# adaLN product by rows of the weights, with a transpose on VectorE, and a reordered beginning

## The chip, the cores and the metric

The kernel runs on one core of a Trainium2 chip. The metric is the device time of one execution in microseconds (us); the median of several executions is compared. The core has TensorE (PE, matmuls; its weight loads are PEld in the profile), VectorE (DVE), ScalarE (ACT), GpSimd (POOL) and SyncE (SP, which here issues most transfers). Each engine works through its own queue in order, and the queues wait for each other through semaphores.

## The reference

One inference step of a small diffusion backbone of two layers on 128 context tokens (prompt) and 128 latent tokens (sample), width 1024, all in float32. Every layer has a token mixer (layer 0 a bidirectional gated recurrence with 8 heads, layer 1 neighbourhood attention) and a mixture of 64 experts with 6 chosen per token. Before each of the four sub-layers stands an RMS norm with adaLN modulation:

```
def _modulation(cvec, ada_w, ada_b):          # cvec: c_ctx for the prompt, c for the sample
    m = silu(cvec) @ ada_w + ada_b            # (1024) @ (1024, 6144)
    return split(m, 6)                        # shift, scale, gate of the mixer; shift, scale, gate of the experts
h = rmsnorm(x, norm_w) * (1 + scale) + shift  # before each sub-layer
x = x + gate * sublayer(h)
```

The change concerns this product (two layers of six parts of 1024 columns, for two condition vectors), and the order in which the first things are loaded and computed.

## The kernel before

Activations lie transposed in SBUF: `xT` and `hT` are 128 partitions x 8 blocks x 256 tokens, and row p*8+k of a width-1024 vector lies on partition p in block k. Weights come through five rooms (`stage`) of 2 MB each, the "stage loads", in a fixed order: four adaLN halves, then the ten 512-column blocks of the recurrence's input projection ("in") with one or two adaLN halves behind each, as the list `ROUNDS` has it, 34 loads in all. SP issues load n as soon as load n-5 has been used (`block_used`). A round is: projection b on PE (`project`), the recurrence's steps that the list puts at its middle and at its end (`recur`), and the adaLN halves (`ada`). The other engines walk through the same list in their own queues. After the rounds come the recurrence's last steps, the output projection (`project_out`), the experts of layer 0 (`experts_front`, `experts`, a loop over 32 pairs of experts), then layer 1.

adaLN part n = (layer, j) is computed in steps:
- A stage load has all 1024 rows of 512 columns (half a part); rows of the load are 2 KB. `ada(n)` on PE multiplies it with the condition vectors (`cond_act`, padded to 32 columns): 8 matmuls of 512 columns, in four column tiles of 32 that each sum two of the eight blocks. All results lie in PSUM bank 7.
- `ada_rows` on ACT copies the bank to `mrow`; PE waits for this (`ada_row`) before the next half.
- When both halves are copied, `ada_columns` on PE turns the row into columns and sums the four tiles: 8 matmuls with 128x128 weights cut from `mrow` and two moving columns (`sel`).
- `modulation` on DVE adds `ada_b` and, for the scale parts, forms the `gain`. The next part's `ada` waits for it (`mod_done`).

In the rounds, `ada_columns` of a part stands in the middle of the projection in a later round (`midway`), and `modulation` stands on DVE between the recurrence's middle and end steps.

The beginning: SP loads both token groups, then every second entry of the list `small` (condition vectors, norm weights, biases, decay bounds, router weights and biases), then stage loads 0 to 4, the table of masks, and after `lb_ps` the states. ACT issues the identity and the other half of `small`. One semaphore counts all of `small`. ACT (Silu of the condition) and PE (transposes of the decay bound logits, `lb_ps`) wait for all of it. PE then sums the squares for the first norm (`norm_sums`) and computes parts 0 and 1; the first projection follows the first norm, which needs these parts. Each matmul in float32 appears in the trace as two records, each with its weight load.

Of the kernel before, what the change touches and what calls it, by code (L numbers as in the profile page):

```python
# [46 lines left out]
C_ID, C_SEL, C_MASKF, C_MASKB, C_BEFORE, C_IOTA, C_WIN, C_WNEG, C_FLIP, C_END = np.cumsum(  # L47
    [0, 128, 2, 128, 32, 128, 4 * SLOTS, 128, 128, 128]).tolist()


def shape_constants():
# [8 lines left out]
    for g in range(4):  # L60
        for s in range(2):
            c[32 * g + s, C_SEL + s] = 1.0
# [9 lines left out]
def build(nc, io):  # L72
    ctx = ExitStack()
    with ctx:
# [106 lines left out]
        mrow = sc(D, (D,))  # L181
# [28 lines left out]
        sel = consts[:, C_SEL:C_SEL + 2]  # L210
# [8 lines left out]
        s_const, s_x, s_small, s_s0 = sem("consts_in"), sem("x_in"), sem("small_in"), sem("states_in")  # L219
        stage_in = [sem(f"stage_in{n}") for n in range(5)]  # L220
# [6 lines left out]
        ada_ps, ada_row, sel_ps, mod_done = sem("ada_in_psum"), sem("ada_rows"), sem("ada_cols_in_psum"), sem("mod_done")  # L227
# [96 lines left out]

        def block_used(n):
# [4 lines left out]
        SMALL = 12 * 16  # L330
# [4 lines left out]
        def heads(a, g):  # L335
# [4 lines left out]
            (cond[:, 0, :], io["c_ctx"].rearrange("(p k) -> p k", p=P)),  # L340
            (cond[:, 1, :], io["c"][0].rearrange("(p k) -> p k", p=P)),
# [5 lines left out]
            (gn_w, io["hgrn_gn_w"].rearrange("a d -> d a")),  # L347
            (router_w[:, 0], io["moe_w_router"][0].rearrange("(p k) e -> p k e", p=P)),
# [4 lines left out]
        assert len(small) * 16 == SMALL  # L353
# [3 lines left out]
        def _(sp):  # L357
            sp.dma_start(x_tok[:, 0, :], io["x_prompt"][0]).then_inc(s_x, 16)
            sp.dma_start(x_tok[:, 1, :], io["x_sample"][0]).then_inc(s_x, 16)
            for dst, src in small[0::2]:  # L360
                sp.dma_start(dst, src).then_inc(s_small, 16)

            def load_stage(n):

                sp.dma_start(stage[rooms[n]], stage_source(stages[n])).then_inc(stage_in[rooms[n]], 16)
# [131 lines left out]
        def _(act):  # L497
            act.dma_start(consts[:, 0:C_MASKF], io["table"][:, 0:C_MASKF]).then_inc(s_const, 16)
            for dst, src in small[1::2]:
# [129 lines left out]
            for b, middle, end, _, adas in ada_rounds():  # L629
# [4 lines left out]
                for n in adas:  # L634
                    ada_rows(n)
# [1090 lines left out]
```

## Time and profile before

| what | value |
|---|---|
| median of the runs | 1677.94 us (3 runs, 1677.0 to 1679.94) |
| the profiled execution: time, span | 1678.47 us, 1676.7 us |
| PE busy | 1604.1 us, 96% of the span |
| weight loads (PEld) | 1150.6 us, 69% |
| DVE, ACT, POOL busy | 468.4, 458.7, 18.6 us |
| mean granted TensorE clock | 0.968 of full speed |
| bytes moved, mean rate | 510.50 MB, 304 GB/s |
| stage loads of ada_w, of the input projection | 24 and 10, of 2048 KB each |
| router loads | weights 2 x 256 KB, biases 2 x 32 KB |

The profile is one execution. Busy time of PE is time in which a matmul was in the pipe, at whatever clock was granted; the clock stands beside it. Times in the rows are from the start of the span.

### The profile page before, as it was taken

The numbers are of one execution on the slowest core, as the hardware profiler recorded it, in microseconds if no ns is written. First come the engines' busy times: TensorE is split into PE (matmuls) and PEld (weight loads), VectorE is DVE, ScalarE is ACT, GpSimd is POOL, SyncE is SP. The second block draws the span as 40 slices with busy tenths as digits, with TensorE's granted clock in tenths as the row PEclk, the third lists the DMA queues.
The fourth block names the chain that finished last, engine by engine and source line by source line (L and its number), as shares of the span: only waits on it lengthen the run. The fifth ranks groups of instructions, "written<-read, shape, count | busy, mean of one in ns | idle before, by whom it ended". The sixth has DMA issues, their size and how long they took to land.

```text
span 1676.7 us, 30416 instructions
## 1 busy us (share of the span) xinstructions
PE 1604.1 (96%) x13039; PEld 1150.6 (69%) x13039; DVE 468.4 (28%) x857; ACT 458.7 (27%) x1055; POOL 18.6 (1%) x25
## 2 busy tenths in 40 slices
PE   5999999989999999999998998989999999999996
PEld 3767866776767767676775775857676767667674
DVE  1035035142222222222222216152222222222224
ACT  2223222231222232222222204132322222222223
POOL 0000000010000000000000000020000000000000
PEclk9999898889999999999999899989999999999999
DMA  9867585663999999999999244237999999999980
GB/s 326 315 240 263 195 284 179 259 226 131 372 389 383 384 388 384 392 385 385 388 383 388 56 151 174 67 163 302 386 381 391 384 391 383 385 387 383 391 340 27
DMA packets 130113, 510.50 MB, mean 304 GB/s; under 512 B 11256, under 2 KB 19600, under 8 KB 97296
## 3 DMA queue, kind: packets, MB, share of 16 engines
q1 hardware_dynamic: 124832, 506.23, 78.5%
q10 hardware_dynamic: 5232, 3.57, 0.7%
q8 instruction: 37, 0.61, 0.1%
q14 instruction: 12, 0.10, 0.0%
HBM read 506.64 MB, written 3.15 MB: 304 GB/s over the span
## 4 chain that ended last, share of the span: by engine, by line
PE 92%; DVE 4%; ACT 3%; DMA 1%; issue 1%; ACTq 0%; DVEq 0%
PE psum L1230 90%; ACT arena L503 1%; PE psum L1551 1%; DMA arena<-in_moe_router_bias 1%; DVE arena L802 0%; DVE arena L844 0%; ACT arena L526 0%; ACTq L500 0%; DVE arena L1064 0%; ACT arena L743 0%; ACT L514 0%; PE psum L1698 0%; DVE arena L804 0%; DVE arena L1123 0%; DVE arena L1119 0%
## 5 line engine op out<-in xcount | busy, mean ns | idle before, releaser
L1230 PE MATMUL psum<-arena 128*64 128x256 f32 (+9 forms) x12756 | 1573.9, 348 | 42.8 <-ACT arena L526 14.3
L1230 PEld LDWEIGHTS psum<-arena 128*64 128x64 f32 (+3 forms) x12756 | 1120.5, 141 | 488.9 <-issue 278.1
L503 ACT ACTIVATE arena<-psum 128x512 f32<-128x512 f32 (+4 forms) x514 | 217.2, 440 | 508.3 <-PE psum L1230 402.6
L1119 DVE TENSOR_TENSOR arena<-psum,arena 128x512 f32<-128x512 f32 x128 | 88.1, 689 | 285.5 <-ACT arena L503 285.5
L503 ACT ACTIVATE arena<-arena 128x512 bf16<-128x512 f32 (+1 forms) x144 | 87.6, 618 | 111.7 <-DVE arena L1119 109.0
L1123 DVE TENSOR_TENSOR arena<-arena 128x512 bf16<-128x512 f32 x128 | 88.7, 693 | 98.1 <-ACT arena L503 98.1
L1110 DVE SCALAR_TENSOR_TENSOR arena<-arena,psum 128x256 f32<-128x256 f32 x64 | 30.8, 482 | 277.6 <-ACT arena L676 277.6
L676 ACT ACTIVATE arena<-psum 128x256 f32<-128x256 f32 x64 | 24.7, 386 | 298.2 <-PE psum L1230 298.2
L1104 DVE COPY arena<-psum 128x512 f32<-128x512 f32 x64 | 44.4, 693 | 136.1 <-PE psum L1230 136.1
L824 DVE TENSOR_TENSOR arena<-psum,arena 128x16 f32<-128x16 f32 x12 | 2.1, 175 | 144.4 <-PE psum L1230 144.4
L844 DVE SCALAR_TENSOR_TENSOR arena<-psum,arena 128x128 f32<-128x128 f32 x64 | 17.7, 344 | 65.3 <-PE psum L1230 65.3
L510 ACT ACTIVATE arena<-arena 128x512 f32<-128x512 f32 x20 | 12.3, 630 | 73.3 <-DVE arena L844 73.2
L492 POOL TENSOR_TENSOR arena<-arena 128x512 f32<-128x512 f32 (+1 forms) x16 | 16.9, 1089 | 1092.9 <-ACT arena L503 1092.8
L1551 PE MATMUL psum<-arena 128*128 128x128 f32 x128 | 25.0, 277 | 2.0 <-DVE arena L1110 2.0
L1031 DVE TENSOR_TENSOR arena<-arena 128x256 bf16<-128x256 f32 x64 | 26.6, 416 | 0.0
L503 ACT ACTIVATION_READ_ACCUMULATOR arena<-psum 64x1 f32 x128 | 25.1, 196 | 0.8
L560 ACT ACTIVATE arena<-psum 128x1024 f32<-128x1024 f32 x8 | 8.2, 1026 | 57.3 <-PE psum L1230 57.3
L526 ACT ACTIVATE arena<-arena 128x128 f32<-128x128 f32 x32 | 12.8, 480 | 12.4 <-DVE arena L804 7.8
L1551 PEld LDWEIGHTS psum<-arena 128*128 128x128 f32 x128 | 13.0, 142 | 2.9 <-DVE arena L1110 2.9
L925 DVE TENSOR_TENSOR arena<-arena 128x1024 f32<-128x1024 f32 x12 | 14.1, 1220 | 0.1
L802 DVE RECIPROCAL arena<-arena 128x256 f32<-128x256 f32 x5 | 8.8, 1754 | 13.8 <-ACT arena L514 13.8
L804 DVE TENSOR_TENSOR arena<-arena 128x512 f32<-128x512 f32 (+1 forms) x15 | 12.1, 865 | 0.2
(137 smaller groups left out, 297.6 us busy)
## 6 DMA issues: line engine op xcount, KB each, us to landing
arena<-in_moe_w_gate SPq DMA_DIRECT2D x64, 2048.0 KB, 9.5
arena<-in_moe_w_up SPq DMA_DIRECT2D x64, 2048.0 KB, 14.1
arena<-in_moe_w_down SPq DMA_DIRECT2D x64, 2048.0 KB, 10.5
arena<-in_ada_w SPq DMA_DIRECT2D x24, 2048.0 KB, 14.9
arena<-in_hgrn_w_in SPq DMA_DIRECT2D x10, 2048.0 KB, 13.6
arena<-in_na_w_qkv SPq DMA_DIRECT2D x6, 2048.0 KB, 19.3
arena<-in_hgrn_w_out SPq DMA_DIRECT2D x1, 4096.0 KB, 13.0
arena<-in_na_w_o SPq DMA_DIRECT2D x1, 4096.0 KB, 14.0
```

Source lines behind the costliest of these rows:

```text
L492: pool.tensor_tensor(out, h_rest[:, a, ks], h_tok[:, part, a, ks], ALU.subtract)\
L503: return act.activation(out, in_, ACT.Copy, **kw)
L676: act.activation(silu[:, j], psum[:, 4, 0:F], ACT.Silu).then_inc(M.silu, 1)
L844: ins = dve.scalar_tensor_tensor(out=xT[:, k, at], in0=psum[:, k // 2, (k % 2) * NT + s * T:(k % 2) * NT + (s + 1) * T], scalar=g[:, k, s: ...
L925: ins = dve.tensor_tensor(dif[d].rearrange("p u (b t) -> p (u b) t", t=size), view, view[:, :, at:at + 1].broadcast_to(shape), ALU.subtract)
L1031: dve.tensor_tensor(onehot[:, j].rearrange("p a (e s) -> p a e s", e=2), slots.unsqueeze(1).unsqueeze(1).broadcast_to(shape), ranks.unsque ...
L1104: dve.tensor_copy(xg[:, j, 4:8], psum[:, 7, :].rearrange("p (k t) -> p k t", t=P)).then_inc(M.xg[1], 1)
L1110: dve.scalar_tensor_tensor(out=hid[:, j], in0=silu[:, j], scalar=slot_w[:, j:j + 1], in1=psum[:, 4, F:2 * F], op0=ALU.mult, op1=ALU.mult). ...
L1119: dve.tensor_tensor(y_rest[:, ds], psum[:, 6 + half, :], y[:, j, 0, ds], ALU.subtract)\
L1123: ins = dve.tensor_tensor(y[:, j, 2, ds], y_rest[:, ds], y[:, j, 1, ds], ALU.subtract)
L1230: return pe.matmul(out, lhsT, rhs, start=start, stop=stop, skip_group_check=True, **kw)
L1551: ins = pe.transpose(psum[:, 5, c * P:(c + 1) * P], hid[:, j, c * P:(c + 1) * P], ident)
```

## The change

It puts the product in another form and moves loads and steps at the beginning:
- A stage load of a half has 512 rows (four of the eight blocks k) of all 1024 columns, in rows of 4 KB. PE multiplies it in 16 matmuls of 256 columns: four column tiles, each with its own quarter of the columns, summed over k in both halves. The sum is complete in 32 partitions x 256 columns per tile.
- `ada_rows`, `ada_columns` and `sel` are gone. DVE transposes bank 7 in blocks of 32x32 into `mod_rows` and adds `ada_b` to two of the 32 columns. PE waits for the transpose (`mod_turned`) before the next part's first half; there is no wait between halves.
- Condition vectors are loaded first, on a semaphore of their own (`s_cond`). All other small loads go to ACT's queue; router weights and biases go to SP's queue behind stage load 9, on `s_router`; the table goes behind load 6 and the states behind load 8 (after `lb_ps`).
- PE transposes the decay bound logits after the first four halves. DVE does the first norm and parts 0 and 1 ahead of the decay bounds, and ACT likewise. PE waits for table and routers ahead of the first router product, DVE for the routers where it adds the bias.

```diff
             if what[0] == "ada":
                 _, l, j, half = what
-                src = io["ada_w"][l, :, j * D + half * BLOCK:j * D + (half + 1) * BLOCK]
+                src = io["ada_w"][l, :, j * D:(j + 1) * D].rearrange("(p k) n -> p k n", p=P)
+                return src[:, half * K // 2:(half + 1) * K // 2]
...
         def _(sp):
+            sp.dma_start(cond[:, 0, :], io["c_ctx"].rearrange("(p k) -> p k", p=P)).then_inc(s_cond, 16)
             sp.dma_start(x_tok[:, 0, :], io["x_prompt"][0]).then_inc(s_x, 16)
             sp.dma_start(x_tok[:, 1, :], io["x_sample"][0]).then_inc(s_x, 16)
-            for dst, src in small[0::2]:
-                sp.dma_start(dst, src).then_inc(s_small, 16)
...
             for n in range(5):
                 load_stage(n)
-            sp.dma_start(consts[:, C_MASKF:], io["table"][:, C_MASKF:]).then_inc(s_table, 16)
-            sp.wait_ge(lb_ps, 1)
-            for d, name in enumerate(("state_hgrn_fwd", "state_hgrn_bwd")):
-                sp.dma_start(s0[:, d], io[name][0, 0].rearrange("h k v -> k h v")).then_inc(s_s0, 16)
             for n in range(5, stages0):
                 sp.wait_ge(*block_used(n - 5))
                 load_stage(n)
+                if n == 6:
+                    sp.dma_start(consts[:, C_MASKF:], io["table"][:, C_MASKF:]).then_inc(s_table, 16)
+                if n == 8:
+                    sp.wait_ge(lb_ps, 1)
+                    for d, name in enumerate(("state_hgrn_fwd", "state_hgrn_bwd")):
+                        sp.dma_start(s0[:, d], io[name][0, 0].rearrange("h k v -> k h v")).then_inc(s_s0, 16)
+                if n == 9:
+                    for dst, src in routers:
+                        sp.dma_start(dst, src).then_inc(s_router, 16)
...
         def _(act):
+            act.dma_start(cond[:, 1, :], io["c"][0].rearrange("(p k) -> p k", p=P)).then_inc(s_cond, 16)
             act.dma_start(consts[:, 0:C_MASKF], io["table"][:, 0:C_MASKF]).then_inc(s_const, 16)
-            for dst, src in small[1::2]:
+            for dst, src in small:
                 act.dma_start(dst, src).then_inc(s_small, 16)
...
-            def ada_rows(n):
-
-                act.wait_ge(ada_ps, n + 1)
-                if n % 2 == 0 and n >= 2:
-                    act.wait_ge(sel_ps, n // 2)
-                copy(mrow[:, (n % 2) * BLOCK:(n % 2 + 1) * BLOCK], psum[:, 7, :]).then_inc(ada_row, 1)
-
-            act.wait_ge(s_small, SMALL)
+            act.wait_ge(s_cond, 32)
             act.wait_ge(ready, 5)
...
             squares(0)
+            norm_root(0)
+            act.wait_ge(s_small, SMALL)
+            norm(0, mod[:, 0, 0])
             act.wait_ge(lb_shift, 1)
             act.activation(lb, lb, ACT.Exp).then_inc(lb_exp, 1)
-            norm_root(0)
-            for n in range(4):
-                ada_rows(n)
-            norm(0, mod[:, 0, 0])
...
             def modulation(n):
 
                 l, j = parts[n]
-                dve.wait_ge(sel_ps, n + 1)
-                dve.tensor_tensor(mod[:, l, j], psum[:, 7, 0:2 * K].rearrange("p (k s) -> p k s", s=2),
+                dve.wait_ge(ada_ps, 2 * n + 2)
+                if n >= 2:
+                    dve.wait_ge(mod_done, n - 1)
+                dve.transpose(mod_rows[:, n % 2],
+                              psum[:, 7, 0:NT].rearrange("p (q k) -> p k q", k=K))\
+                   .then_inc(mod_turned, 1)
+                dve.wait_ge(mod_turned, n + 1)
+                dve.tensor_tensor(mod[:, l, j], mod_rows[:, n % 2, :, 0:2],
                                   ada_b[:, l, j].unsqueeze(2).broadcast_to((P, K, 2)), ALU.add).then_inc(mod_done, 1)
...
             def ada(n):
 
                 w = staged()
-                if n % 2:
-                    pe.wait_ge(ada_row, n)
-                elif n:
-                    pe.wait_ge(mod_done, n // 2)
-                for i in range(K // 4):
+                part, half = n // 2, n % 2
+                if half == 0 and part:
+                    pe.wait_ge(mod_turned, part)
+                for i in range(K // 2):
                     for c in range(4):
-                        ins = mm(psum[32 * c:32 * c + 32, 7, :], cond_act[:, 4 * i + c, :], w[:, 4 * i + c, :],
-                                 i == 0, i == K // 4 - 1)
+                        ins = mm(psum[32 * c:32 * c + 32, 7, 0:NT], cond_act[:, half * K // 2 + i, :],
+                                 w[:, i, c * NT:(c + 1) * NT], half == 0 and i == 0, half == 1 and i == K // 2 - 1)
                 ins.then_inc(ada_ps, 1)
 
-            def ada_columns(n):
-
-                pe.wait_ge(ada_row, 2 * n + 2)
-                for k in range(K):
-                    ins = mm(psum[:, 7, 2 * k:2 * k + 2], mrow[:, k::K], sel, True, True)
-                ins.then_inc(sel_ps, 1)
-
-            for n in range(2):
-                ada(2 * n)
-                ada(2 * n + 1)
-                ada_columns(n)
-            pe.wait_ge(s_table, 16)
+            for n in range(4):
+                ada(n)
+            pe.wait_ge(s_small, SMALL)
+            for i in range(3):
+                ins = pe.transpose(psum[:, 5, i * HEADS:(i + 1) * HEADS], lbrow[0:HEADS, i], ident[0:HEADS, 0:HEADS])
+            ins.then_inc(lb_ps, 1)
...
                         recur(g, item)
-                    if part is not None:
-                        ada_columns(part)
...
+            pe.wait_ge(s_table, 16)
+            pe.wait_ge(s_router, ROUTER)
             experts_front(0)
```

## Rows read from the trace of the kernel before

**Rows 1.** Windows: length, busy PE PEld DVE ACT POOL (count), clock, DMA share, GB/s.
```profile
2.00:14.00 12.00, 3.65 (x16) 3.28 (x16) 1.61 (x3) 1.28 (x1) 0.23 (x2) 1.00 1.00 285
14.00:36.00 22.00, 14.86 (x67) 10.26 (x68) 5.94 (x14) 7.84 (x13) 0.00 (x0) 1.00 1.04 386
48.55:295.19 246.64, 243.05 (x1521) 177.57 (x1521) 75.00 (x106) 66.55 (x86) 0.00 (x0) 0.91 0.68 245
48.55:64.80 16.25, 16.25 (x68) 13.63 (x72) 1.17 (x5) 3.45 (x7) 0.00 (x0) 0.86 1.02 376
64.80:80.70 15.90, 15.90 (x85) 12.53 (x88) 0.00 (x0) 1.62 (x2) 0.00 (x0) 1.00 0.78 274
500.00:600.00 100.00, 100.00 (x972) 69.82 (x970) 25.11 (x42) 27.65 (x72) 0.00 (x0) 1.00 0.98 388
```

**Rows 2.** Chain of waits, 0 to 60 us: start, length, what.
```profile
6.12 11.62 DMA arena<-in_moe_router_bias
...
29.06 1.96 PE psum L1230 x16
...
31.70 3.98 PE psum L1230 x16
...
36.02 3.61 PE psum L1230 x16
...
48.55 11.51 PE psum L1230 x42
```

**Rows 3.** The fifth stage load (first projection): issue time, and time to landing.
```profile
L365 SPq DMA_DIRECT2D arena<-in_hgrn_w_in x1: 5295/5295/5295, 20.3 to 20.3; - x1
...
DMA to landing us min/median/max: 20.1/20.1/20.1
```

**Rows 4.** Windows: behind the third columns; the first and last low-clock columns.
```profile
94.10:97.50 3.40, 3.40 (x10) 2.72 (x9) 3.33 (x10) 1.06 (x1) 0.00 (x0) 0.51 0.02 4
139.50:143.50 4.00, 4.00 (x19) 4.00 (x18) 0.04 (x1) 0.00 (x0) 0.00 (x0) 0.78 1.05 387
...
275.20:279.20 4.00, 4.00 (x26) 3.99 (x18) 0.00 (x0) 0.00 (x0) 0.00 (x0) 0.89 1.05 391
```

**Rows 5.** Groups by form, PE, 48.55 to 295.19 us: busy, mean | idle before.
```profile
L1230 PE MATMUL psum<-arena 128*32 128x512 f32 x273 | 33.3, 598 | 1.6 <-ACT arena L503 1.6
L1230 PE MATMUL psum<-arena 128*128 128x2 f32 x128 | 30.9, 372 | 0.2 <-PE psum L1369 0.2
L1230 PE MATMUL psum<-arena 128*128 128x128 f32 x80 | 9.9, 278 | 1.8 <-DVE arena L969 1.8
```

**Rows 6.** Timeline of PEld in the second projection: start, length, what.
```profile
66.59 13.68 PEld L1230 LDWEIGHTS psum<-arena 128*128 128x128 f32 x64 [0.84 <-issue]
```

**Rows 7.** Timeline of PEld in an expert's gate and up product.
```profile
707.38 6.62 PEld L1230 LDWEIGHTS psum<-arena 128*64 128x64 f32 x62 [0.29 <-issue]
```

**Rows 8.** Groups by form, PEld and DVE, beginning to the output projection.
```profile
L1230 PEld LDWEIGHTS psum<-arena 128*32 128x32 f32 x768 | 15.7, 111 | 30.6 <-issue 30.2
L824 DVE TENSOR_TENSOR arena<-psum,arena 128x16 f32<-128x16 f32 x12 | 2.1, 175 | 144.4 <-PE psum L1230 144.4
L802 DVE RECIPROCAL arena<-arena 128x256 f32<-128x256 f32 x1 | 1.8, 1754 | 3.3 <-ACT arena L514 3.3
L964 DVE TENSOR_TENSOR arena<-psum,arena 128x256 f32<-128x256 f32 x2 | 0.8, 414 | 0.0
```

**Rows 9.** Chain of waits, 295 to 320 us.
```profile
295.26 1.90 PE psum L1230 x16
...
297.83 3.98 PE psum L1230 x16
...
302.16 3.65 PE psum L1230 x16
...
307.74 1.11 ACT arena L619
...
308.88 1.28 ACT L622
...
310.17 1.06 ACT arena L622
...
312.82 7.59 PE psum L1230 x28
```

More of the change, by code:

```diff
@@ L44 @@
 BLOCK_W = K * BLOCK
-C_ID, C_SEL, C_MASKF, C_MASKB, C_BEFORE, C_IOTA, C_WIN, C_WNEG, C_FLIP, C_END = np.cumsum(
-    [0, 128, 2, 128, 32, 128, 4 * SLOTS, 128, 128, 128]).tolist()
+C_ID, C_MASKF, C_MASKB, C_BEFORE, C_IOTA, C_WIN, C_WNEG, C_FLIP, C_END = np.cumsum(
+    [0, 128, 128, 32, 128, 4 * SLOTS, 128, 128, 128]).tolist()
 def shape_constants():
@@ L59, in shape_constants @@
     c[:, C_IOTA:C_IOTA + 4 * SLOTS] = np.arange(4 * SLOTS)[None, :]
-    for g in range(4):
-        for s in range(2):
-            c[32 * g + s, C_SEL + s] = 1.0
     start = np.clip(np.arange(GRID_W) - WIN_C // 2, 0, GRID_W - WIN_C)
@@ L180, in build @@
         scan_keep = sc(UNITS * T)
-        mrow = sc(D, (D,))
+        mod_rows = sc(2 * K * 32, (2, K, 32))
         x_tok = cut(2 * D, (2, D), at=scratch_at)
@@ L209, in build @@
         before = consts[:, C_BEFORE:C_BEFORE + P]
-        sel = consts[:, C_SEL:C_SEL + 2]
         window = consts[:, C_WIN:C_WIN + P]
@@ L219, in build @@
         s_const, s_x, s_small, s_s0 = sem("consts_in"), sem("x_in"), sem("small_in"), sem("states_in")
+        s_cond, s_router = sem("cond_in"), sem("routers_in")
         stage_in = [sem(f"stage_in{n}") for n in range(5)]
@@ L226, in build @@
         cond_done = sem("cond_act_done")
-        ada_ps, ada_row, sel_ps, mod_done = sem("ada_in_psum"), sem("ada_rows"), sem("ada_cols_in_psum"), sem("mod_done")
+        ada_ps, mod_turned, mod_done = sem("ada_in_psum"), sem("mod_turned"), sem("mod_done")
         sq_done, ssum, root = sem("squares"), sem("square_sums"), sem("root")
@@ L323, in build, with stage_room @@
         room_count = [rooms[:n + 1].count(rooms[n]) for n in range(len(rooms))]
+        def stage_room(n):
+            room = stage[rooms[n]]
+            if stages[n][0] == "ada":
+                return room.rearrange("p k n -> p (k n)").rearrange("p (k n) -> p k n", n=D)
+            return room
         def block_used(n):
@@ L328, in block_used @@
             return (ada_ps, ada_n) if stages[n][0] == "ada" else (proj, n + 1 - ada_n)
-        SMALL = 12 * 16
+        SMALL, ROUTER = 6 * 16, 4 * 16
         def bank(n, count=1):
@@ L347, in build @@
             (gn_w, io["hgrn_gn_w"].rearrange("a d -> d a")),
+        ]
+        routers = [
             (router_w[:, 0], io["moe_w_router"][0].rearrange("(p k) e -> p k e", p=P)),
@@ L352, in build @@
         ]
-        assert len(small) * 16 == SMALL
+        assert (len(small) * 16, len(routers) * 16) == (SMALL, ROUTER)
         @block.sync
         def _(sp):
+            sp.dma_start(cond[:, 0, :], io["c_ctx"].rearrange("(p k) -> p k", p=P)).then_inc(s_cond, 16)
             sp.dma_start(x_tok[:, 0, :], io["x_prompt"][0]).then_inc(s_x, 16)
             sp.dma_start(x_tok[:, 1, :], io["x_sample"][0]).then_inc(s_x, 16)
-            for dst, src in small[0::2]:
-                sp.dma_start(dst, src).then_inc(s_small, 16)
             def load_stage(n):
-                sp.dma_start(stage[rooms[n]], stage_source(stages[n])).then_inc(stage_in[rooms[n]], 16)
+                sp.dma_start(stage_room(n), stage_source(stages[n])).then_inc(stage_in[rooms[n]], 16)
             def load_gate_up(m, j, expert):
@@ L627, in recur @@
                     state_out(g, 1)
-            for b, middle, end, _, adas in ada_rounds():
+            for b, middle, end, _, _ in ada_rounds():
                 for g, item in middle + end:
@@ L633, in _ @@
                     project(b)
-                for n in adas:
-                    ada_rows(n)
             def experts_front(m):
@@ L855, in _ @@
                                 psum[:, n, :].rearrange("p (k t) -> p k t", t=T)).then_inc(x_sb, 1)
+            normed(0)
             dve.wait_ge(s_small, SMALL)
+            modulation(0)
+            modulation(1)
+            gains_ready(0)
+            norm(0, mod[:, 0, 0])
             dve.wait_ge(lb_ps, 1)
@@ L868, in _ @@
             link(dve.tensor_scalar(one_minus_lb, lb0, -1.0, 1.0, ALU.mult, ALU.add))
-            normed(0)
-            modulation(0)
-            modulation(1)
-            gains_ready(0)
-            norm(0, mod[:, 0, 0])
             dve.wait_ge(s_table, 16)
@@ L1042, in experts_front @@
                 dve.wait_ge(M.scores, 1)
+                dve.wait_ge(s_router, ROUTER)
                 link(dve.tensor_tensor(selv, scores, router_b[:, m].unsqueeze(1).broadcast_to((P, 2, E)), ALU.add))
@@ L1238, in _ @@
                 ins.then_inc(x_ps, 1)
-            pe.wait_ge(s_small, SMALL)
-            for i in range(3):
-                ins = pe.transpose(psum[:, 5, i * HEADS:(i + 1) * HEADS], lbrow[0:HEADS, i], ident[0:HEADS, 0:HEADS])
-            ins.then_inc(lb_ps, 1)
             pe.wait_ge(ready, 5)
@@ L1398, in recur @@
                     state(g, 1)
-            for b, middle, end, part, adas in ada_rounds():
+            for b, middle, end, _, adas in ada_rounds():
                 def midway():
```

4 lines of the change are left out of this document (1 added, 3 removed).

## The prediction

> **What bounds the kernel now.** I read the windows by stage first, to see which engine is full where. In the expert stretches TensorE (PE) is busy for all of 100 us at a granted clock of 1.00 while transfers run at 388 GB/s [rows 1]: there PE sets the pace, and what comes earlier in time only shifts it. The change touches the first 319 us alone, so the question is what ends last there. From 48.55 us (first matmul of the first projection) to 295.19 us PE is busy for 243.05 of 246.64 us, but at a mean clock of 0.91, and the DMA engines only for 0.68 of the time [rows 1]. That stretch is PE's too, so PE time taken out of it is gained, as long as transfers don't take over.
>
> Next the chain of waits in order of time, for the beginning [rows 2]. The first conditioning matmuls wait for the last router bias (11.62 us); then each adaLN part goes PE, ScalarE (ACT) copy, PE, VectorE (DVE). The last step on PE, the "columns" product, takes 3.98 us for 16 matmuls of two columns each. The first projection starts at 48.55, although its weights, the fifth stage load, were there at 20.3 + 20.1 = 40.4 us [rows 3].
>
> Last, the granted clock around the columns [rows 4]. The stretch 94.1 to 97.5, which follows the columns of the third part, was at 0.51, so at the 1.2 GHz level; a round with a conditioning half and no columns (64.8 to 80.7) was at 1.00 [rows 1].
>
> **The change, part by part.** The profiled execution took 1678.47 us (span 1676.7), 0.5 above the median of the runs shown; sums go from it.
>
> *Columns removed.* Between 48.55 and 295.19 there were 128 two-column records, 16 for each of 8 parts [rows 5]. One set lies on the chain for 3.98 us [rows 2]. PE has no other work in that time, so all is gained: 8 x 3.98 = 31.8 us. The other four sets lie in the beginning and the tail, below.
>
> *Clock given back.* A mean of 0.91 means that 18% of 246.64 us, 44.4 us, were at half clock; half of that, 22.2 us, is lost. The first projection's own share stays (0.86 over 16.25 us: 4.6 us low, 2.3 lost [rows 1]), since PE will still have been mostly idle before it. In four of the eight column stretches the low clock already began under the columns (0.78 for the first, 0.89 for the last; together 6.3 us, 3.1 of loss) [rows 4], and that time is counted with the columns. Left: 22.2 - 2.3 - 3.1 = 16.8 us. Rounding of 0.91 makes it 15.6 to 18.0.
>
> *Row copies removed.* Two halves stood directly behind each other in two of these rounds and waited for the ACT copy: 1.6 us. PE also waited 1.8 us for the score mask, because the ACT decay exponentials were queued behind a row copy, and 0.2 before a column set [rows 5]. Together 3.6 us; those exponentials no longer have a row copy ahead of them.
>
> *The new product.* A half is now 16 matmuls of 256 columns instead of 8 of 512, each recorded as two. Four column tiles ran side by side before: 16 records of 512 took 1.90 us [rows 9]. At full clock a 256-column record takes 13.68 / 64 = 0.214 us [rows 6]; 32 of them in four tiles are 8 x 0.214 = 1.71 us, and the same remainder of 0.19 gives 1.90 again: zero. The new thing is twice as many weight loads, with half the time to hide each. The nearest row is the expert product, also 256 columns, in two tiles: 62 loads in 6.62 us, 0.214 us per pair [rows 7], so loads of twice the width are hidden there. I take zero. Above: 768 loads of this form were busy 15.7 us [rows 8], and the new product has 24 x 32 = 768: +15.7 us if all of them stood open, +7.9 for the added half. Below zero nothing: the streamed columns are the same in number.
> The Trainium skill, "TensorE: Matmul & The Clock Gate", Part 3, section "The mechanism", says that a weight load overlaps with matmuls in flight only when its row group differs. Here all four tiles use all rows, so by that rule the loads would stand open and the forecast would rise to about 1621; the expert row speaks against it.
>
> *The DVE transpose.* Not in the trace. 128x256 out of PSUM took 0.414 us as a product; the dearest DVE operation of that size, the reciprocal, 1.754, and the small add that it joins 0.175 [rows 8]. I take 0.41 and keep 0.2 to 1.75. It adds a DVE step between one part and the next part's first half, but DVE sat idle before every modulation, 144.4 us over 12 [rows 8], and both halves of a part are now ready a round before DVE comes to it. So it costs nothing in the rounds. DVE work behind it (decays, output copies) starts no later, since the wait for the columns is gone. It is on the path twice: before the first projection and in the tail.
>
> *The beginning.* Condition vectors come on a semaphore of their own, so ACT no longer waits until 17.7 us; the decay bounds leave the path. What ends last is then the fifth stage load. Four router transfers (0.59 MB) leave the queue ahead of it: 1.5 us at 386 GB/s. From 2 to 14 us only 285 GB/s were moved, a loss of 3.1 us against 386 [rows 1]; the small vectors, ada_b above all, stay, so I give back 1.2. It lands at 40.4 - 2.7 = 37.7 (35.8 to 40.4). The other arm: the fourth load lands one load (5.4 us) earlier, at 32.3; a half takes 1.9 to 3.6 us by clock [rows 2]; from the last columns to the first projection it took 1.6 us, now 2.0 with the transpose: 36.2 to 37.9. So the first projection starts at about 38.1 instead of 48.55: 10.4 us (8 to 12.5). The rows of ada_w are now read 4 KB at a time instead of 2 KB; 2 KB rows already moved 386 GB/s [rows 1], so nothing for that.
> Moved behind stages 6, 8 and 9 on SP's queue: table, states, router weights. States are wanted in the sixth round, routers past 320 us. DVE waits for the table ahead of its first decay step, which comes with the third round, near 72 us; behind loads 5 and 6 the table lands near 37.7 + 2 x 5.4 + 1.2 = 50 us. SP now waits for lb_ps behind load 8, but load 9 needs the first projection to end in any case. PE meets the table and router waits only ahead of the first router product.
>
> *The tail* (from 295.2 until the output projection, at about 318.7, where the state ends within the last chain row) loses two column sets and three row copies [rows 9]. New chain: half 1.9, transpose and wake 0.6, half 1.9 (DVE's add, gain and output copy lie beside it), ACT's square 1.1, sums 1.7, Ln 1.11, table 1.28, Exp 1.06, copy 0.6, key turn 0.7, copy 0.6, state 0.9: 13.4 us instead of 23.5. Short idle gaps remain and the clock may fall in them, so I take 10.0 (7 to 12). The last transfer needed, 4 MB of output weights, is issued ahead of this stretch and lands well within it.
>
> *Do transfers take over?* A full round loads 6.29 MB, 16.3 us at 386 GB/s; PE needs 15.9 + 1.9 = 17.8 us [rows 1, 9] and more with recurrence work. PE stays last, by 1.5 us.
>
> Sum: 10.4 + 31.8 + 16.8 + 3.6 + 10.0 = 72.6 us. 1678.5 - 72.6 = 1605.9; less 0.5 for the median: **1605**.
>
> **The rivals.**
> (a) *Open weight loads*: 7.9 to 15.7 us given back, 1613 to 1621. For it: twice the loads. Against it: the expert product. Chance 0.09.
> (b) *Transfers pace the rounds*: if loads fall under 6.29 MB / 17.8 us = 353 GB/s, as in the first 14 us, the two rounds without recurrence work stretch first. At 330 a round is 19.1 us; with a late fifth load some 8 us in all: 1613. Chance 0.07.
> (c) *The low clock belongs to the recurrence matmuls* and stays: 16.8 us are not gained, 1622. For it: from the fourth part on, columns and recurrence lie close together. Against it: the fall at 94.1 had no recurrence before it. Chance 0.09.
> (d) *Slower*: the four tiles no longer run side by side, because they now stream different columns under the same condition weights. A half then takes 32 x 0.214 = 6.84 us instead of 1.90, over 24 halves 118 us: 1723. It decides the sign from 72.6 / 24 = 3.0 us more per half on. Against it: tiles ran together before with different columns each. Chance 0.03.
> (e) *The reordering does nothing*, the first projection waits as long as before, and half of (c) holds: 1624. Chance 0.02.
>
> **How the numbers follow.** The forecast has 0.68, with a range of its own of 1597 to 1613 from the bounds of beginning, tail and clock. A measurement of this kernel can tell about 0.2%, 3.4 us, from no change. Cases (a), (b), (c) and (e) are all faster. Faster: 0.68 + 0.09 + 0.07 + 0.09 + 0.02 = 0.95; slower 0.03 from (d); the 0.02 left is within 0.2%, several of these at once. For 8 in 10 I go from 1595 (all lower bounds nearly met) to 1622.
>
> **What would show it.** Right: no two-column matmuls; halves of about 1.9 us; first projection near 38 us; clock near 1.00 from there to the tail; output projection near 245 us; experts unchanged, only earlier. (a) would show as halves of 2.2 to 2.6 us, (b) as PE waiting for ada_w or hgrn_w_in, (c) as stretches at 0.5 after scores, (d) as halves of 5 us or more. The forecast is wrong if the expert stretch itself changes in length.

## The result, and the profile after

The changed kernel takes 1606.09 us (median of 4 runs, 1605.86 to 1609.95) where the kernel before takes 1678.32 in the same series (4 runs, 1677.0 to 1679.94): 0.9575 of the time, with a 95% interval of 0.9558 to 0.9591. The profiled execution took 1606.1 us, with a span of 1604.2. The forecast was 1605.

First the page: the granted clock in 40 slices of the span, each about 40 us. In the first seven, which hold the beginning, the rounds and the tail, it is now nine tenths or more throughout.

```profile
PEclk9999999899999999999998999899999999999998
```

Then the windows, with the columns of [rows 1]: the loading stretch, the beginning, all from the first projection to the last half before the tail, and the first projection alone.

```profile
2.00:14.00 12.00, 3.65 (x16) 3.28 (x16) 1.61 (x3) 0.34 (x1) 0.23 (x2) 1.00 1.00 354
14.00:36.00 22.00, 15.26 (x147) 9.72 (x147) 5.86 (x10) 6.33 (x11) 0.00 (x0) 0.92 1.05 390
36.77:229.85 193.08, 192.92 (x1664) 144.08 (x1665) 79.81 (x123) 58.13 (x71) 0.00 (x0) 1.00 0.87 327
36.77:53.00 16.23, 16.22 (x97) 13.01 (x97) 2.62 (x14) 5.97 (x10) 0.00 (x0) 1.00 1.03 397
```

The stage that took 246.64 us at a clock of 0.91 takes 193.08 at 1.00, and TensorE stands for only 0.16 us in it. What TensorE did there, by forms (count, busy us, mean ns, idle before), after and, in the second fence, the lines of before that [rows 5] leave out:

```profile
L1236 PE MATMUL psum<-arena 128*128 128x256 f32 x512 | 113.8, 381 | 2.0 <-ACT arena L535 1.8
L1236 PE MATMUL psum<-arena 128*32 128x256 f32 x544 | 32.6, 381 | 0.0
L1236 PE MATMUL psum<-arena 128*128 128x512 f32 x68 | 30.3, 598 | 0.0
L1236 PE MATMUL psum<-arena 128*128 128x128 f32 x80 | 9.8, 277 | 0.0
```
```profile
L1230 PE MATMUL psum<-arena 128*128 128x256 f32 x512 | 129.5, 418 | 1.6 <-ACT arena L526 1.6
L1230 PE MATMUL psum<-arena 128*128 128x512 f32 x68 | 34.8, 667 | 0.0
```

The two-column group of 30.9 us is gone. The projections' 512 records took 129.5 us and now take 113.8, the 68 wide ones 34.8 and 30.3, the product's own 33.3 [rows 5] and 32.6: the same work, 20.9 us less, which is the clock. Records of neighbouring forms overlap, so these sums come out somewhat high: the stage's busy time fell by 243.05 - 192.92 = 50.1 us, which leaves 19.2 beside the 30.9 of the two-column group.

The beginning, as the chain of waits (start, length, what), and under it the stage loads that SyncE issued in the first 40 us (the issue of the first load of the projection, and the longest time to landing, which is its own):

```profile
3.90 8.58 ACTq L509
...
12.51 16.43 DMA arena<-in_hgrn_gn_w
...
28.96 0.46 DVE arena L825
...
29.56 5.12 PE psum L1236 x61
...
34.70 0.46 DVE arena L825
...
36.77 0.67 PE psum L1236 x2
```
```profile
L368 SPq DMA_DIRECT2D arena<-in_hgrn_w_in x3: 1678/2532/5152, 8.5 to 38.0; - x3
...
DMA to landing us min/median/max: 10.3/19.2/27.0
```

The chain is not the one that was forecast. The fifth load was there at 8.5 + 27.0 = 35.5 us, but the first projection, at 36.77, was held by a chain that starts from a small load: ScalarE's queue spent 8.58 us on issuing the decay bound logits, so the last of the small loads, `gn_w`, was issued at 12.51 and landed at 28.94. VectorE waits for all small loads ahead of its first transpose, and TensorE for this transpose ahead of the third half.

The tail, as TensorE's timeline (start, length, idle before it and who ended it):

```profile
229.85 1.94 PE L1236 MATMUL psum<-arena 128*32 128x256 f32 x32
232.45 1.94 PE L1236 MATMUL psum<-arena 128*32 128x256 f32 x32 [0.67 <-DVE arena L825]
235.13 4.75 PE L1236 MATMUL psum<-arena 128*128 128x512 f32 x44 [0.74 <-ACT arena L615]
241.18 0.66 PE L1364 MATMUL psum<-arena 128*128 128x128 f32 x4 [1.30 <-ACT arena L512]
242.52 1.16 PE L1236 MATMUL psum<-arena 128*128 128x128 f32 x8 [0.69 <-ACT arena L512]
```

A half stands in it alone: 32 records in 1.94 us. The output projection follows at 243.7.

Last a line that should not have changed: ScalarE's 32 SiLUs of layer 0's pairs of experts (duration min/median/max in ns, start of the first and last), before and after.

```profile
L676 ACT ACTIVATE arena<-psum x32: 385/386/386, 399.2 to 909.9; 128x256 f32<-128x256 f32 x32
```
```profile
L675 ACT ACTIVATE arena<-psum x32: 383/383/384, 323.2 to 835.0; 128x256 f32<-128x256 f32 x32
```

The first pair comes 76.0 us earlier, the last 74.9: with the same instructions and no wait the pairs take longer. From start to start it is 16.287 us before and 16.321 after (mean of the 60 undisturbed steps of both layers). So some of the gain is given back where nothing was changed.

### The profile page after: what moved, and what is told of

It reads as the page before. It is cut to its first block, busy times and chain, and to the rows that moved or that the text cites. A ratio compares the mean times of both kernels' runs of the same rounds, so it can differ in the third digit from the quotient of the medians.

```text
span 1604.2 us, 30774 instructions
## 1 busy us (share of the span) xinstructions
PE 1536.1 (96%) x13231; PEld 1105.4 (69%) x13231; DVE 474.3 (30%) x869; ACT 444.2 (28%) x1031; POOL 19.8 (1%) x25
## 4 chain that ended last, share of the span: by engine, by line
PE 91%; DVE 4%; ACT 2%; issue 1%; DMA 1%; ACTq 1%; DVEq 0%
PE psum L1236 90%; DMA arena<-in_hgrn_gn_w 1%; PE psum L1544 1%; ACT arena L512 1%; ACTq L509 1%; DVE arena L801 0%; DVE arena L849 0%; ACT arena L535 0%; ACT arena L742 0%; ACT L523 0%; PE psum L1693 0%; DVE arena L803 0%; DVE arena L1129 0%; DVE arena L1125 0%; DVE arena L1070 0%
## 5 line engine op out<-in xcount | busy, mean ns | idle before, releaser
L1236 PE MATMUL psum<-arena 128*64 128x256 f32 (+8 forms) x12948 | 1506.5, 340 | 45.6 <-ACT arena L535 14.7
L1236 PEld LDWEIGHTS psum<-arena 128*64 128x64 f32 (+4 forms) x12948 | 1076.0, 136 | 469.1 <-issue 259.3
L512 ACT ACTIVATE arena<-psum 128x512 bf16<-128x512 f32 (+4 forms) x490 | 202.5, 431 | 452.8 <-PE psum L1236 342.1
L519 ACT ACTIVATE arena<-arena 128x512 f32<-128x512 f32 x20 | 12.3, 628 | 72.6 <-DVE arena L849 72.6
L825 DVE STREAM_TRANSPOSE arena<-psum 128x256 f32<-128x256 f32 x12 | 5.4, 447 | 63.5 <-PE psum L1236 54.1
L535 ACT ACTIVATE arena<-arena 128x128 f32<-128x128 f32 x32 | 12.7, 480 | 19.8 <-DVEq L841 12.0
```

The source lines that it names most:

```text
L512: return act.activation(out, in_, ACT.Copy, **kw)
L1236: return pe.matmul(out, lhsT, rhs, start=start, stop=stop, skip_group_check=True, **kw)
```

## The experiments

**The reordering alone.** The old product, with the loads and steps of the beginning in the new order.

```diff
+            sp.dma_start(cond[:, 0, :], io["c_ctx"]...).then_inc(s_cond, 16)
...
-            act.wait_ge(s_small, SMALL)
+            act.wait_ge(s_cond, 32)
             act.wait_ge(ready, 5)
...
             for n in range(2):
                 ada(2 * n)
                 ada(2 * n + 1)
                 ada_columns(n)
```

> The kernel before with the reordered beginning alone; the old product with its twelve sets of two-column matmuls stays. Theory (the two-column sets and the low clock behind them carry the gain): the condition no longer waits for the router bias, so the first four halves run as their weights land (fourth load at about 28.8 us in the profile of after), and behind the fourth stand its own 2 to 4 us, the row copy, a set of two-column matmuls of 3.98 us, the sum and the norm: first projection at 39 to 42 us where before had 48.55, so 7 to 9 us gained, about 1669 to 1671 us, and the twelve low-clock stretches stay. Rival (the order of the loads also thins the rounds, since the row copies and the queue are free earlier): more than 15 us gained, under 1663 us. Rival (the beginning is bound by the fifth load and nothing else): first projection at 36 us, 12.5 us gained, 1665 us.

1671.75 us, 0.9961 of before (0.9950 to 0.9973): 6.9 us gained, just short of the theory's 7 to 9. Chain of waits:

```profile
22.67 3.98 PE psum L1238 x16
...
31.50 3.68 PE psum L1238 x16
...
35.85 3.98 PE psum L1238 x16
...
41.43 10.71 PE psum L1238 x38
```

The first projection starts at 41.43, held by the second set of two-column matmuls. Both rivals fall. Pairs of experts take 16.287 us here.

**The product alone.** The new product with the old order of the loads.

```diff
-            sp.dma_start(cond[:, 0, :], io["c_ctx"]...).then_inc(s_cond, 16)
+            for dst, src in small[0::2]:
+                sp.dma_start(dst, src).then_inc(s_small, 16)
...
-            act.wait_ge(s_cond, 32)
+            act.wait_ge(s_small, SMALL)
```

> The new product with the old order of the loads. Theory: the condition is ready at 29.06 us, as before; then four halves of 2 us with two transposes of 0.46 us behind them, the gains and the norm: first projection at 40 to 41.5 us, where the fifth load lands at about 40.4 us; all that follows is as in the changed kernel. That is 3.5 to 5 us over the changed kernel's 36.77, so about 1610 us. The sum of the gains of the two parts made alone is then larger than that of both together, since each shortens the same beginning. Rival (the parts add): the reordering's 10.4 us of the prediction are missing as a whole, 1616 us.

1609.81 us, 0.9593 of before (0.9575 to 0.9612). The time fits, the reason does not quite: the first projection started at 38.51, and the chain shows that it was held by the table of masks, which the old order loads and awaits ahead of it.

```profile
17.80 20.67 DMA arena<-in_table
...
38.51 21.70 PE psum L1229 x110
```

The product alone gains 68.9 us, the reordering alone 6.9, both 72.2: they share the beginning. On top of the new product the reordering is worth 3.7 us, and the two intervals overlap. In the profile of the product alone the first projection runs at a clock of 0.84 (38.51 to 55.00 us), which costs 2.6 us; in the changed kernel it runs at 1.00.

**Two-column matmuls put back.** The changed kernel with eight added matmuls in the middle of each of eight projections.

```diff
                 def midway():
                     for g, item in middle:
                         recur(g, item)
+                    if part is not None and b is not None:
+                        flat = hT.rearrange("p k t -> p (k t)")
+                        for k in range(K):
+                            mm(psum[:, 2 * (b % 2) + 1, 2 * k:2 * k + 2], flat[:, k:D:K], ident[:, 0:2], True, True)
```

> The changed kernel with eight added matmuls of two columns against 128x128 weights read with a stride, in the middle of each of the eight projections of rounds 2 to 9, where before had its sets (their result is overwritten by the projection). No transpose, copy or wait goes with them. Theory (the sets cost their own 3.98 us and pull the clock down behind them, in before 16.8 us over twelve sets or 1.4 us a set): 8 x 3.98 = 31.8 plus 8 x 1.4 = 11.2 us, so about 1649 us, with low-clock stretches behind the sets and a mean clock near 0.975. Rival (the low clock belonged to the matmuls of the recurrence or to the waits for the row copies, which are not back): 31.8 us alone, 1638 us, with the clock at 1.00 from 36 to 285 us. Rival (the cost was in the waits around the sets): under 1625 us.

**Full matmuls in the same places.**

```diff
+                    if part is not None and b is not None:
+                        for k in range(9):
+                            mm(psum[:, 2 * (b % 2) + 1, 0:NT], hT[:, k % K, 0:T], hT[:, k % K], True, True)
```

> The changed kernel with nine added matmuls of 256 columns against 128x128 weights in the same eight places (their result is overwritten), about as long as a set of the kernel before: 9 x 0.43 = 3.9 us. Theory (only two-column matmuls pull the clock down): 8 x 3.9 = 31 us, about 1637 us, with the clock at 1.00 from 36 to 285 us; together with the kernel that has the two-column sets this gives the clock's part, about 11 us. Rival (any work added there brings a low clock, as it changes when the others wait): low-clock stretches here too, 1645 us or more.

1656.01 us with the two-column sets (0.9864 of before, 0.9838 to 0.9890), 1641.32 with the full ones (0.9776, 0.9755 to 0.9797): 49.9 and 35.2 us over the changed kernel, for added work of the same length. TensorE's windows (length, busy, clock, DMA share, GB/s), first with two-column sets, at and behind the first two of them, then with full matmuls in the same stretches:

```profile
78.00:82.00 4.00, 4.00 (x18) 1.00 1.02 403
82.00:86.00 4.00, 4.00 (x12) 0.57 0.31 126
98.00:102.00 4.00, 4.00 (x15) 1.00 1.05 390
102.00:110.00 8.00, 8.00 (x18) 0.57 0.71 281
```
```profile
82.00:86.00 4.00, 4.00 (x21) 1.00 0.38 152
102.00:110.00 8.00, 8.00 (x28) 1.00 0.49 195
139.29:142.75 3.46, 0.01 (x1) 1.00 1.01 388
143.00:147.00 4.00, 4.00 (x12) 0.57 1.06 393
```

Behind the two-column sets the clock is at its 1.2 GHz level, 0.57 in the mean of 4 and of 8 us, so low for 3.4 and 6.9 us of them. All eight sets have such a stretch behind them. TensorE shows as busy all the time; what it did before the fall was the two-column matmuls. Behind the full matmuls it stays up. The one fall there follows a different event, a stand of 3.46 us in which TensorE waited for nothing that the profile shows. The forms say what the clock cost with the two-column sets (first projection to the tail):

```profile
L1236 PE MATMUL psum<-arena 128*128 128x256 f32 x512 | 126.5, 410 | 3.7 <-ACT arena L535 1.9 <-issue 1.8
L1236 PE MATMUL psum<-arena 128*128 128x512 f32 x68 | 36.3, 692 | 0.0
...
L1236 PE MATMUL psum<-arena 128*128 128x2 f32 x128 | 30.9, 372 | 0.1
```

Against the changed kernel the projections take 12.7 us more and the wide matmuls 6.0, beside the 30.9 of the sets themselves: 18.7 us for eight sets, 2.3 a set. By the stage's busy time (240.95 us from 38.45 to 281.39, against 192.92) it is 48.0 - 30.9 = 17.1 us, 2.1 a set. Expected were 1.4, but that came from dividing the prediction's 16.8 us by twelve sets, where they had been counted over the eight of this stage: 2.1 a set, as here. The theory holds; that the low clock belongs to the recurrence falls, since the recurrence is the same in both. The sets differ from the full matmuls in two ways, though: two columns instead of 256, and weights read with a stride of eight, as in the kernel before. Which of the two the clock follows was not separated. Of the 35.2 us of the full matmuls 3.5 are the unexplained stand, and up to 2 the low clock behind it; the rest, 30, is the 72 matmuls.

**One strip after another.** The same matmuls of a half, in another order.

```diff
-                for i in range(K // 2):
-                    for c in range(4):
+                for c in range(4):
+                    for i in range(K // 2):
```

> The changed kernel with the matmuls of a half in another order: four in a row on one strip of 32 columns, then the next strip, instead of one strip after another each time. The same matmuls and the same number. Theory (a half takes 1.94 us because the four strips work side by side; one behind another a half takes the four to one, at most 16 x 0.427 = 6.84 us): 20 halves of the rounds and the tail with 4.9 us more, 98 us, and 1 to 4 us in the beginning, about 1705 us. Rival (the order of issue doesn't matter, since the array takes the strips side by side from its queue anyway): 1606 us. Rival (weight loads are what keeps a half at its length, and with one strip after another they are open as well): above 1723 us.

1661.02 us (0.9907 of before, 0.9886 to 0.9928). Both the theory's number and the rivals miss. A half in the tail, on TensorE's timeline:

```profile
280.87 4.60 PE L1236 MATMUL psum<-arena 128*32 128x256 f32 x32
```

4.60 us, between 1.94 and 6.84. The order of issue counts, and changing the strip with every matmul is worth 2.66 us a half. This half starts 51.0 us later than in the changed kernel (229.85): 17 halves between the first projection and this point make about 45.2 us of it, and the later start (42.77 against 36.77 us) the rest. Why four in a row on one strip still overlap in part was not tested.

**The old places of the tiles.** The new product needs no selection columns, so the constants are two columns shorter and all tiles behind them lie 8 bytes earlier in SBUF. Here the two words stay, unused.

```diff
         consts = cut(C_END)
+        cut(2)
```

> The changed kernel with two unused words left behind the constants, where the two selection columns were, so that every tile behind them (expert weights, tokens, scratch) lies where it lay before. The trace of before and that of the kernel with only the reordered beginning show 16.287 us for a pair of experts; the changed kernel and all three others that carry the new product show 16.321, with the same instructions. The new product's constants are two columns shorter, which moves all later tiles by 8 bytes. Theory (the 0.034 us a pair comes from the places of the tiles): pairs at 16.287 us, 62 x 0.034 = 2.1 us in the pairs and some 0.5 us between the layers, so about 1603.5 us. Rival (it comes from what else the new product brings, its instructions or the time at which the loads run): pairs stay at 16.32 and the time at 1606.

**The same, at even places.**

```diff
         consts = cut(C_END)
+        cut(2)
...
+        cut(3)
         ring_at = top[0]
```

> As the one with the old places, and three more words left in front of the expert weights, so that these and the scratch begin at a multiple of 64 bytes (44 bytes past one in the changed kernel, 52 in the kernel before). Theory (places matter by where they stand in such a block): pairs differ from 16.321 and from 16.287, shorter if tiles that begin a block are read best, by at most some 0.1 us a pair or 6 us in all. Rival (only the difference between 44 and 52 matters by chance, or the places play no part): 16.29 to 16.32 and 1603.5 to 1606 us.

**Only the weights and the scratch at their old places.**

```diff
+        cut(2)
         ring_at = top[0]
```

> The changed kernel with two unused words directly in front of the expert weights, so that these, the second weight area and the scratch lie where they lay in the kernel before, while the small tiles between the constants and the weights (condition, gains, routers, identity in bf16) stay 8 bytes earlier. Theory (it is the place of the weights and the scratch, which the expert matmuls read): pairs of experts at 16.287 us. Rival (it is the place of the small tiles): pairs at 16.321 us.

1602.28 us (0.9546 of before, 0.9533 to 0.9559) with the old places, 1601.56 (0.9536, 0.9523 to 0.9549) with the even ones, 1602.24 in a single run with only the weights and the scratch put back. The lines of the SiLUs of layer 0, in this order:

```profile
L676 ACT ACTIVATE arena<-psum x32: 385/385/386, 325.0 to 835.8; 128x256 f32<-128x256 f32 x32
```
```profile
L677 ACT ACTIVATE arena<-psum x32: 383/383/384, 325.9 to 836.0; 128x256 f32<-128x256 f32 x32
```
```profile
L676 ACT ACTIVATE arena<-psum x32: 387/387/387, 324.1 to 834.9; 128x256 f32<-128x256 f32 x32
```

510.8, 510.1 and 510.8 us from the first to the last, where the changed kernel has 511.8. From start to start that is 16.287, 16.265 and 16.287 us. So the change of length follows the place of the weights and the scratch, counted from the start of the arena: 44 bytes past a multiple of 64 in the changed kernel (16.321), 52 in the kernel before (16.287), 0 with the even places (16.265). Only these three places were tried. All fourteen kernels agree with it: four at 52 bytes, the reordering alone among them, have 16.287, seven at 44 have 16.320 or 16.321, three at 0 have 16.264 or 16.265. Which operand of which matmul reads slower was not separated. The whole kernels gained more (3.8 and 4.5 us by the medians) than the 62 steps explain (2.1 and 3.5); the rest is not assigned.

**The beginning without the small loads ahead of the transpose.**

```diff
             normed(0)
-            dve.wait_ge(s_small, SMALL)
-            modulation(0)
+            modulation(0, lambda: dve.wait_ge(s_small, SMALL))
```

> The changed kernel with VectorE's wait for the small loads moved from ahead of its first transpose to behind it, ahead of the sum that needs the loads. In the changed kernel the first transpose starts at 28.96 us, when the last small load has landed (28.94), and TensorE stands for 2.71 us before the third half. Theory: the first transpose follows the second half at about 27 us, the fourth half ends about 2 us after the fourth load (28.8), and the first projection starts when the fifth load has landed, 35.5 to 36 us instead of 36.77: 0.8 to 1.3 us gained, about 1605 us. Rival (the small loads then hold the sums, and the gains and the norm behind them stand where they were): first projection at 36.5 to 37 us, no gain.

1605.71 us (0.9566 of before, 0.9553 to 0.9579), no gain that can be told. The first projection started as the theory says, at 35.85, when its weights had landed. But now TensorE had stood idle for them, first on its timeline, and its windows (length, busy, clock, DMA share, GB/s) show what followed:

```profile
35.85 10.35 PE L1236 MATMUL psum<-arena 128*128 128x256 f32 x39 [3.34 <-DMA arena<-in_hgrn_w_in]
```
```profile
36.00:39.00 3.00, 3.00 (x8) 0.50 1.01 399
244.00:248.00 4.00, 4.00 (x15) 0.57 0.99 413
```

Three microseconds at half clock took 1.5 us back; the second low stretch is one that the changed kernel's profile does not have. In the changed kernel the low stretch lies ahead of that, in the third and fourth half (0.92 over 14 to 36 us), and the projection starts at 1.00. What the start gains, the clock costs.

**The tail in another order.** In the first round without a projection, the recurrence's sums go ahead of the 23rd half, and VectorE's copy ahead of its transpose.

```diff
+                last = end == [(1, 4)]
+                if last:
+                    recur(1, 4)
                 for n in adas[:1]:
                     ada(n)
-                for g, item in end:
+                for g, item in [] if last else end:
                     recur(g, item)
```

> The changed kernel with another order in the first of the three rounds without a projection: the group's output sums and states come ahead of the 23rd half, and VectorE's copy for them ahead of its transpose. Theory: TensorE's waits of 0.67, 0.74 and 1.30 us in that stretch (2.7 us) shrink to 0.4 us, since the two last halves then lie beside the row norm on ScalarE; the wait of 0.69 us ahead of the last states stays. 2.0 to 2.4 us gained, about 1603.8 us. Rival (the chain through ScalarE sets the end of the stretch, not TensorE's order): the same wait appears ahead of the second turn of the keys, no gain.

1602.95 us (0.9548 of before, 0.9535 to 0.9561). TensorE's timeline:

```profile
231.42 8.51 PE L1239 MATMUL psum<-arena 128*32 128x256 f32 x108
239.87 0.66 PE L1367 MATMUL psum<-arena 128*128 128x128 f32 x4
241.21 5.10 PE L1239 MATMUL psum<-arena 128*128 128x128 f32 x24 [0.69 <-ACT arena L512]
```

From the 22nd half to the last states 9.79 us instead of 12.67: three of the four waits are gone, one remains. 2.9 us against an expected 2.0 to 2.4. In the whole time the gain is 3.1 us by the medians, but the interval just touches that of the changed kernel, so the tail's own length is what shows it.

**Together.** The new tail with the even places, and these with the changed wait in the beginning.

```diff
+        cut(2)
...
+        cut(3)
         ring_at = top[0]
...
+                if last:
+                    recur(1, 4)
```

> The changed kernel with the new order in the tail and with the tiles at multiples of 64 bytes. Each alone gained 3 to 4.5 us. Theory (they lie in different stages and add): pairs of experts at 16.265 us, waits in the tail at 0.7 us, about 1599 us. Rival (a gain in front of the experts is eaten by their weights, which then land too late): about 1601.5 us, with waits for weights in front of the first pair.

```diff
-            dve.wait_ge(s_small, SMALL)
-            modulation(0)
+            modulation(0, lambda: dve.wait_ge(s_small, SMALL))
```

> The same, with VectorE's wait for the small loads behind its first transpose as well. That alone let the first projection start at 35.85 us, but TensorE's clock was then at its low level until about 39 us, and the time was the same as the changed kernel's. Theory (the low clock takes back what the earlier start gives): within 1 us of the kernel with the tail and the places alone. Rival (the start counts): 1.5 to 2.5 us less than it.

1599.04 us (0.9541 of before, 0.9525 to 0.9556) and 1597.31 (0.9527, 0.9513 to 0.9540). The first two gains add; the pairs take 16.265 us in both. The third is inconclusive: 1.7 us less by the medians, with intervals that overlap. The last kernel beats both the kernel before (by 4.7%) and the changed one, whose interval begins at 0.9558.

## Why the prediction was right, point by point

The total was forecast at 72.6 us of the profiled execution, and 72.5 came. That it agrees so closely is partly chance: what was gained up to the end of the output projection came to 4 us more than forecast, and 4 us were lost behind it, where none was expected.

- *Columns* (31.8): 128 records of 30.9 us gone. Right.
- *Clock* (16.8): 19.2 us by the busy time of the stage, 20.9 by the forms. 2.3 of it is the first projection's own low clock, which the forecast let stand because TensorE would still have been idle before it. It was not: the third and fourth half ran shortly ahead of it, and it ran at 1.00 (the window from 36.77). The 16.9 that are left by the busy time are the 16.8 of the forecast, 2.1 us a set. The sets' part was right; the first projection's part was wrongly left out.
- *Row copies* (3.6): idle time of the stage fell from 3.59 to 0.16 us. Right. Columns, clock and row copies together were forecast at 52.2; the stage became 246.64 - 193.08 = 53.6 shorter.
- *New product* (0): a half takes 1.94 us against 1.90 [rows 9]. The weight loads were hidden, as the expert row suggested [rows 7]: TensorE was busy without a break in this stage. The Trainium skill, "TensorE: Matmul & The Clock Gate", Part 3, "The mechanism", has a load overlap only where the row group differs. The trace does not agree with this sentence, since all four strips here use all rows, and the time by that rule, 1621, did not come. The same section of the Trainium skill also lets a load into the background weight buffer go ahead of matmuls in flight; no run here can tell whether that is what happened.
- *Transpose* (0.41): 0.46 in the chain, 447 ns mean on the page. Right, and invisible in the rounds.
- *Beginning* (10.4): 48.55 - 36.77 = 11.8. The number fits, a step failed: "the small vectors, ada_b above all, stay" priced them as bytes only. The transfers moved 354 GB/s in the first 14 us, where I gave back less, so the fifth load was early (35.5, not 37.7). What the sum did not have is ScalarE's queue, to which the change moves every small load: its 8.58 us issue set the time of the last one, and so of VectorE's wait. In seven other kernels with this beginning the first projection started at 38.3 to 38.5, with the small loads late: the profiled execution was an early one, and 10.1 is the usual gain. Nor does the gain need the reordering, to which the sum credits it: the product alone, with the old loads, starts the first projection at 38.51.
- *Tail* (10.0): 23.5 to 13.85 us, 9.65. Right; the four waits of 3.4 us in it are the "short idle gaps", and the new order takes 2.9 of them.
- *Not in the sum*: the output projection ran at a clock of 0.89 before (318 to 340 us) and at 1.00 after, 1.65 us more.
- *Experts unchanged, only earlier*: wrong. This is the step that failed, and the forecast named it as what would make it wrong. Of 76.6 us saved at the end of the output projection, 0.6 went ahead of the first pair, 2.1 in the 62 steps between pairs of both layers, 0.5 between the layers and 0.9 at the end. The 2.1 are the tiles' places, shown by three kernels. The 0.5 and 0.9 moved both ways from kernel to kernel (between the layers 221.8 to 224.3 us); their cause stays open.

Of the rivals, (a), the open loads, falls with 1.94 us; (b), the pace of transfers, with 0.16 us of idle time at 327 GB/s; (c), the recurrence's clock, with the pair of kernels above; (e), the useless reordering, with the first projection at 36.77 and the 6.9 us that the reordering gains alone; what it adds on top of the new product is not clear of the noise. (d), strips no longer side by side, can be made by the order of the matmuls. It then costs 2.66 us a half and not the 4.9 that were priced, and stays under the 3.0 from which it would decide the sign: 1661 us, still faster than before.

## What to carry to other kernels

Matmuls of two columns are not cheap: eight of them took 3.9 us here, as long as nine of 256 columns, and 2.1 to 2.3 us more by the clock behind them; look for both before weighing other forms. A gain in a stage comes through in full only if everything behind it stays where it was, so compare the length of a part that nobody touched; tiles that shift by a few bytes can lengthen it. When loads are moved to another queue, count what each takes to issue there, and who waits for the last of them.

## What the runs showed of the hardware

- The start of the expert weights and scratch in SBUF changes TensorE's pace while it is busy throughout: 16.265, 16.287 and 16.321 us a pair at 0, 52 and 44 bytes past a multiple of 64, from the start of the arena.
- TensorE's clock falls to 1.2 GHz behind sets of two-column matmuls though the engine shows as busy (0.57 in the windows), and not behind as many microseconds of 256-column ones (1.00). The weights of the sets were also read with a stride, which was not tried apart.
- Loads of 32 columns' weights are hidden under matmuls of 256 columns on other strips of the same rows (32 records in 1.94 us); with four in a row on one strip a half takes 4.60 us.
- One DMA of the decay bound logits held ScalarE's queue for 8.58 us, and the one of `gn_w` behind it, issued at 12.51, took 16.43 us to land. With the reordering alone, and the same order on this queue, the first was issued in 3.84 us; why it takes longer beside the new product's loads was not tested.
- TensorE stood twice for 1.8 and 3.5 us in the two kernels with added matmuls, with no releaser in the trace; the cause was not found.
